# A two-layer backbone step: square sums between the spreads, late weights split in place, filler matmuls, and an earlier store

## The reference, cut to what matters

```python
for l in range(2):                                   # the same code for 128 context and 256 latent tokens
    h = rmsnorm(x) * (1 + scale1) + shift1
    q, k, v, xr, gr, ga, gb = split(h @ w_in)        # 5632 columns
    att = attention(q, k, v)                         # 8 heads of 128
    rnn = gelu(gr) * bidirectional_rg_lru(conv(xr))
    merged = sigmoid(ga) * (att @ w_attn_proj) + sigmoid(gb) * (rnn @ w_rnn_proj)
    x = x + gate1 * (merged @ w_out)
    h2 = rmsnorm(x) * (1 + scale2) + shift2
    x = x + gate2 * moe(h2)                          # 16 experts, top 2 in the best group of 4
y = rmsnorm(x) * final_norm_g
```

## Time and profile before

| what | value |
|---|---|
| median of 3 runs | 1584.49 us |
| the profiled execution | 1587.41 us, of it the span 1585.5 us |
| PE busy | 1485.0 us, 94% of the span |
| PEld, DVE, ACT, POOL busy | 75%, 70%, 58%, 10% |
| mean granted TensorE clock | 0.967 |
| chain that ended last | PE 79%, DVE 7%, ACT 4%, issue 4%, DMA 4%, POOL 1% |
| DMA, mean over the span | 235 GB/s |

### The profile page before, as it was taken

The page is one execution under the profiler, slowest core; times in us unless marked ns, Lnnn a source line. Parts: engine busy times, 40 slices in busy tenths (PEclk is TensorE's granted clock), DMA queues, the critical chain, the costliest instruction groups (busy, mean ns, idle before and its releaser), DMA issues.

```text
span 1585.5 us, 19352 instructions
## 1 busy us (share of the span) xinstructions
PE 1485.0 (94%) x7317; PEld 1195.4 (75%) x7317; DVE 1116.2 (70%) x1709; ACT 926.0 (58%) x1174; POOL 153.3 (10%) x209
## 2 busy tenths in 40 slices
PE   6999999989996999999979999999899599999996
PEld 3699866669875788888748998665898378888885
DVE  4447656765646999999852665776564689999996
ACT  1333579962224877778742245899321467787874
POOL 0100012200010000000230000221000200000002
PEclk8999999989997999999989999999899699999999
DMA  9455422124656999999744554112340789999993
GB/s 349 163 199 203 153 103 101 62 102 166 212 193 253 358 406 408 409 408 404 278 162 154 186 199 161 62 62 90 128 160 1 279 311 407 413 411 410 408 357 121
DMA packets 132708, 373.01 MB, mean 235 GB/s; under 512 B 9216, under 2 KB 12672, under 8 KB 132608
## 3 DMA queue, kind: packets, MB, share of 16 engines
q1 hardware_dynamic: 113728, 326.57, 54.9%
q0 software_dynamic: 10432, 25.18, 4.5%
q10 hardware_dynamic: 8448, 19.94, 3.2%
HBM read 351.71 MB, written 19.94 MB: 234 GB/s over the span
## 4 chain that ended last, share of the span: by engine, by line
PE 79%; DVE 7%; ACT 4%; issue 4%; DMA 4%; POOL 1%; SPq 0%; POOLq 0%; DVEq 0%; ACTq 0%
PE bank L522 24%; PE bank L820 19%; PE bank L511 10%; PE bank L826 10%; PE bank L532 2%; PE bank L712 2%; PE bank L792 2%; DMA ring<-in_w_ada 1%; PE bank L685 1%; PE bank L548 1%; DMA expert_rows<-gb 1%; PE bank L541 1%; PE bank L622 1%; PE bank L617 1%; DMA tmp<-expert_rows,posu 1%
## 5 line engine op out<-in xcount | busy, mean ns | idle before, releaser
L1838 DVE TENSOR_TENSOR spot_low<-spot,piece_high 128x2048 fp32r<-128x2048 f32 x192 | 434.1, 2287 | 32.8 <-ACT piece_high L1226 31.5
L1226 ACT ACTIVATE piece_high<-spot 128x2048 fp32r<-128x2048 f32 x192 | 366.9, 1917 | 46.6 <-PE bank L826 45.4
L820 PE MATMUL bank<-piece_high,ga_r 128*128 128x512 f32 x768 | 310.9, 405 | 4.7 <-ACT ga_r L1231 2.2
L820 PE MATMUL bank<-spot_low,ga_r 128*128 128x512 f32 x768 | 303.7, 395 | 0.0
L826 PE MATMUL bank<-piece_high,ga_r 128*128 128x512 f32 x768 | 211.6, 397 | 0.0
L511 PE MATMUL bank<-hT,ring 128*128 128x384 f32 x576 | 198.0, 499 | 9.6 <-ACT hT L1041 6.5
L522 PE MATMUL bank<-parts_r,ga_r 128*128 128x384 f32 x768 | 202.6, 345 | 0.0
L820 PEld LDWEIGHTS bank<-piece_high,ga_r 128*128 128x128 f32 x768 | 145.6, 190 | 39.0 <-ACT ga_r L1231 3.0
L511 PEld LDWEIGHTS bank<-hT,ring 128*128 128x128 f32 x576 | 109.2, 195 | 82.6 <-issue 11.3
L826 PEld LDWEIGHTS bank<-piece_high,ga_r 128*128 128x128 f32 x768 | 145.1, 189 | 34.8
L820 PEld LDWEIGHTS bank<-spot_low,ga_r 128*128 128x128 f32 x768 | 145.9, 190 | 31.0
(11 more groups left out here) (308 smaller groups left out, 2289.3 us busy)
## 6 DMA issues: line engine op xcount, KB each, us to landing
spot<-in_w_gate_up SPq DMA_DIRECT2D x128, 1024.0 KB, 8.0
spot<-in_w_down SPq DMA_DIRECT2D x64, 1024.0 KB, 8.3
ring<-in_w_ada SPq DMA_DIRECT2D x24, 2048.0 KB, 8.0
ring<-in_w_in SPq DMA_DIRECT2D x22, 2048.0 KB, 8.0
expert_rows<-gb ACTq DMA_DIRECT2D x28, 512.0 KB, 7.3
ring<-in_w_attn_proj SPq DMA_DIRECT2D x4, 2048.0 KB, 8.6
ring<-in_w_rnn_proj SPq DMA_DIRECT2D x4, 2048.0 KB, 8.3
ring<-in_w_out SPq DMA_DIRECT2D x4, 2048.0 KB, 8.0
```

The costliest lines, as they stand in the source:

```text
L820: pe.matmul(out[n], high[:, 2 * q + k, :], w[:, k, n * 512:(n + 1) * 512], start=(q == 0 and k == 0 and i == 0), stop=False)
L1226: ac.activation(highs[p % HIGHS], spots[u], ACT.Copy).then_inc(S("piece_high"), 1)
L1838: ve.tensor_tensor(spots_low[u], spots[u], highs[p % HIGHS].bitcast(F32), ALU.subtract)\
```

## The change

Six edits, five of them in both layers.

1. Late weights: the high part goes to one of four buffers (`spare` and three in `hT`), the low part is written over the chunk in its ring slot. `xc` is no longer used. A ring slot of a late chunk is released when the last product with it has ended, not when its low part is written.
2. End of attention: the first late high part moves into the loop, `lru_tables(15)` and `lru_root(15)` move behind `att_copy(23)` and the second high part; on DVE `one_minus_square(15)` moves behind the second low part.
3. `run_on`: ten float32 matmuls per layer into a bank that nobody reads: two of 384 columns before the ranks, four of 512 before `ids`, three before `xturn(0)`, one behind it.
4. Last expert: `copy_y(13)` and `store_y(13)` stand ahead of the high part of gate_up's last piece. `low_of(0)` stands between the combinations of rows, `low_of(1)` behind them.
5. Layer 0's tail: the squares and their sums stand ahead of the branch, the sum of group g - 3 behind the spread of group g. In the branch the squares are made again after each further block (a sixth PE step).
6. Layer 1's chunk "kv", and with it all loads behind it on SP, waits for the square sums (`ss_done`).

```diff
+LAG = 3
+LATE_HIGHS = 4
...
-                   [(part(hTf, 0), part(hTf, 1)), (part(hTf, 2), part(spare_r, 0)), (part(xcf, 0), part(xcf, 1))]]
+        late_high = [part(spare_r, 0)] + [part(hTf, i) for i in range(LATE_HIGHS - 1)]
+        ring_r = sb_r("ring")
...
-        def w_part(kind, n):
+        def w_high_part(kind, n):
 
             at = SPLIT_AT[kind, n]
-            return w_parts[at // EARLY][at % EARLY % PAIRS_OF_PARTS]
+            return w_parts[at % PAIRS_OF_PARTS][0] if at < EARLY else late_high[at % LATE_HIGHS]
+
+        def w_low_part(l, kind, n):
+
+            at = SPLIT_AT[kind, n]
+            if at < EARLY:
+                return w_parts[at % PAIRS_OF_PARTS][1]
+            s = CHUNK_SLOT[CHUNK_AT[(l, f"{kind}{n // 4}")]][0]
+            return ring_r[:, s, :].rearrange("p (k n) -> p k n", k=KT)[:, :, n % 4 * P:(n % 4 + 1) * P]
...
-                if g[1:] in SPLIT_AT:
+                if SPLIT_AT.get(g[1:], EARLY) < EARLY:
                     return S("w_low"), split_no(*g) + 1
             return S("gemm_done"), G_AT[g] + 1
...
+                if l and name == "kv":
+                    sy.wait_ge(S("ss_done"), 2 * l + 1)
...
+            def run_on(bank, times, width=512):
+
+                for _ in range(times):
+                    pe.matmul(bank[:, 0:width], ident, con[:, 256:256 + width], start=True, stop=True)
...
+                run_on(SB[1], 2, T)
                 bank = t_take((l, "rank", 0))
...
+                run_on(SB[1], 4)
                 bank = t_take((l, "ids", 0))
...
+                run_on(SB[1], 3)
                 xturn(0)
+                run_on(SB[1], 1)
...
                     mm.then_inc(S("group_done"), 1)
+                    if l + 1 < DEPTH and g >= LAG:
+                        square_sum(hT, g - LAG, slice(0, T), sq_base + KT + g - LAG + 1)
+                if l + 1 < DEPTH:
+                    for g in range(KT - LAG, KT):
+                        mm = square_sum(hT, g, slice(0, T), sq_base + KT + g + 1)
+                    mm.then_inc(S("ss_done"), 1)
...
                 one_more(0)
 
                 if l + 1 < DEPTH:
-                    for g in range(KT):
-                        mm = square_sum(hT, g, slice(0, T), sq_base + KT + g + 1)
-                    mm.then_inc(S("ss_done"), 1)
                     continue
...
+                    if i == 3 * KT - 1:
+                        high_part(EARLY)
...
-                    if i >= KT:
+                    if KT <= i < 3 * KT - 1:
                         lru_tables(i - KT)
                     if i >= 1:
                         att_copy(i - 1)
-                lru_root(15)
-                high_part(EARLY)
                 att_copy(23)
                 high_part(EARLY + 1)
+                lru_tables(15)
+                lru_root(15)
...
-                    piece_high(f"gu{e}", 3)
+                    if e < NE - 1:
+                        piece_high(f"gu{e}", 3)
                     if e >= 2:
                         copy_y(e - 2)
+                    if e == NE - 1:
+                        store_y(e - 2)
+                        piece_high(f"gu{e}", 3)
...
-                ac.activation(smx[:, 0, 7:8], ones[:, 0:1], ACT.Sqrt)
                 ac.wait_ge(S("blocks_known"), l + 1)
                 more = ac.value_load(nri[0:1, 0:1], min_val=0, max_val=MORE)
+                x_steps = 6 if l + 1 < DEPTH else 5
+                if l + 1 < DEPTH:
+                    for g in range(KT):
+                        ac.wait_ge(S("group_added"), l * KT + g + 1)
+                        ac.activation(hT[:, g, :], xT[:, g, :], ACT.Square).then_inc(S("sq_ready"), 1)
...
                 one_more(0)
+                ac.activation(smx[:, 0, 7:8], ones[:, 0:1], ACT.Sqrt)
...
-                one_minus_square(15)
                 low_part(EARLY)
                 att_split(HEADS - 1)
                 low_part(EARLY + 1)
+                one_minus_square(15)
                 scan(15)
...
-                for i in range(HELD):
-                    ve.wait_ge(S("y_copied"), l * NE + SENT + i + 1)
-                    low_of(i, (SB_pair, G_pair)[i], slot_gate[:, SENT + i:SENT + i + 1]).then_inc(S("held_low"), 1)
+                    if t:
+                        i = t - 1
+                        ve.wait_ge(S("y_copied"), l * NE + SENT + i + 1)
+                        low_of(i, (SB_pair, G_pair)[i], slot_gate[:, SENT + i:SENT + i + 1]).then_inc(S("held_low"), 1)
```

44 lines of the change are left out of this document (25 added, 19 removed).

## The result

The changed kernel takes 1569.68 us in the median of four runs (1568.08 to 1571.1). The kernel before took 1584.05 us in the same set (four runs, 1583.37 to 1587.31). The ratio is 0.9905, its 95% interval 0.9887 to 0.9923: 14.4 us are won where 24.5 were forecast, and the time lies 1.7 us outside the range of 1556.5 to 1568. The profiled execution took 1571.1 us, with a span of 1569.2 us against 1585.5 before. The 16.3 us between the two spans are what the traces can explain. The other 2 us are spread between executions: the profile of before lay 3.4 us over the median of this set, this one 1.4 us over its own.

The account below looks back on a forecast made before the run. PE is four fifths of the chain, so time is won only where it waits or runs at low clock. 10.4 + 7.65 + 1.75 + 4.7 = 24.5 us off 1587.41, less 2.9, gives 1560.0; eight in ten: 1556.5 to 1568.

Parts of the forecast that it names:

- End of attention: Late weights and reordered end of attention: first late product 4.4 us earlier, third 5.2 per layer, 10.4 us in all.
- the wait of 1.6 us: Ahead of the third late product, PE waits for its low part, delayed on DVE behind `scan(15)`: 1.6 us given back.
- Fillers: Routing and first expert: filler matmuls off the path keep PE's clock up, 4.3 + 3.35 = 7.65 us.
- lower bound of 2.7: Routing and first expert: if the fillers run cold and delay the first expert, 1.8 + 0.9 = 2.7 us remain.
- Edit 4: Layer tails: earlier store of expert 13 and moved `low_of` bring rows and spread sooner, 1.75 us per layer.
- Squares, sums and loads: Layer 0's tail: sums among the spreads, keys start at 813.9 when held weights land: 4.7 us, including 1.75 from the store.
- The sign that I had named: Ahead of layer 1's keys: PE waiting for a DMA would show the forecast right.
- (a): First expert: clock falls just as it starts, 4.55 us lost from the sum, 1564.6 us; chance 0.2.
- (b): End of attention gives little, half its gain lost: 5.2 us less, 1565.2 us; chance 0.12.
- (c): Late weight stream stalls PE 2.5 us per hand-over from landings of 16 us on; about 1611 us; chance 0.03.
- (d): Layer 0's tail gives nothing, its load landing in 13 us instead of 8: 1564.7 us; chance 0.05.
- The sign for "wrong" that I had named: Whole kernel: a total gain under 16 us would show the forecast wrong.

Follow-up runs that it names:

- run 5: Changed kernel without the ten filler matmuls per layer; 1569.9 us, ratio 0.9915 to the kernel before.
- run 6: Changed kernel with the old order at the end of attention, late weights still split in place with four high buffers; 1576.37 us, ratio 0.9959 to the kernel before.
- run 9: Changed kernel with DVE's low parts of expert 14's down and expert 15's pieces written in two half instructions; 1563.27 us, ratio 0.987 to the kernel before.
- run 10: Run 9 with expert 13's copy and store also put back where they stood before; 1561.69 us, ratio 0.9865 to the kernel before.
- run 11: Changed kernel with four filler matmuls between the last down product and the first transposes of both tails; 1565.46 us, ratio 0.9887 to the kernel before.
- run 12: Run 10 with five fillers instead of four ahead of `ids`; 1559.27 us, ratio 0.9852 to the kernel before.
- run 1: Changed kernel with expert 13's copy and store and both `low_of` put back where they stood; 1567.05 us, ratio 0.9903 to the kernel before.
- run 2: Changed kernel with only expert 13's copy and store put back where they stood; 1563.52 us, ratio 0.989 to the kernel before.
- run 3: Changed kernel with only both `low_of` put back behind the three combinations; 1567.41 us, ratio 0.9913 to the kernel before.
- run 4: Changed kernel with layer 1's loads no longer waiting for the square sums; 1568.31 us, ratio 0.9908 to the kernel before.
- run 7: Changed kernel with squares and sums behind the branch again, the loads' wait for the sums kept; 1571.86 us, ratio 0.9929 to the kernel before.
- run 8: Changed kernel with squares and sums behind the branch again and loads not waiting for the sums; 1574.39 us, ratio 0.9946 to the kernel before.

## Why the prediction was wrong

- **End of attention: right at its first step, a little high behind it.** The first late product came 4.3 us earlier (4.4 forecast). The 0.8 us more behind it aren't steady: +0.7 in layer 0, -0.4 in layer 1, where the clock fell behind a wait of 2.23 us that it had stood before. With 8.95 us for both layers it was within its bounds (8.8 to 11). The way there was partly another: the wait of 1.6 us that I forecast ahead of the third product never came, because the first product ran at half clock (granted 0.50 from 336 to 339, 5.6 us in place of 4.2) and the third low part was ready at 345.91, when PE came to it at 345.98.
- **Fillers: right in mechanism, in size partly by luck.** Layer 1 gave 3.3 us (3.35 forecast). Layer 0 gave 2.6 in the profile of the changed kernel, close to the lower bound of 2.7 that I had worked out for cold fillers, and 4.2 in the other traces (4.3 forecast). But 1.7 of those 4.2 run 5 has without any filler; against run 5 they bring 2.5 us in layer 0. I took it that none of them lies on the path, and in most traces the cold third group does, by about 0.9 us.
- **Edit 4: this step failed.** I wrote that with the store moved ahead "the six gathers behind it: the last rows land at 789.2 instead of 790.95", and so 1.75 us per layer. The rows came 1.9 us later against the experts instead, PE's wait grew from 1.97 to 3.83 us, and the transposes behind it ran cold: -2.7 and -2.0 us, and -0.7 in the spreads of layer 1. Of the 8.2 us between the two spans and my sum, this step is 8.9; the other steps make up for 0.7. I shifted the chain behind the store as a block, with each duration as it stood. Three of the six durations (those that start at 776.22, 782.68 and 784.96) were not the gathers' own but held waits for DVE, and in the page nothing said so: their release is given as "issue". Nor did I ask what the pushed-back high part does to DVE's list: it alone ends the first gather 0.7 us later. I also let the wait of PE grow or shrink without asking for the clock behind it, though I had done so everywhere else.
- **Squares, sums and loads: right in sign, sized by a wait that isn't there.** The weights were never held (I misread where the wait stands), so the keys were not bound by a load at 813.9; 5.3 us came behind the spread where 2.95 were forecast. The sign that I had named, PE waiting for a DMA ahead of the keys, didn't show; PE waited 5.65 us for ACT. The 5.5 us from the root to the keys were right (5.46).
- **Not priced: the square root's table in layer 1's tail.** With its preload behind the branch no other table is loaded in between, and the load of 1.28 us in the final norm is gone: 1.3 us won.
- **Rivals.** None of the four was it. (a) was wrong: the clock was up in the first expert, though it had fallen ahead of it. (b) was 12% and the end of attention gave 8.95 of 10.4. (c) didn't come: the weight stream never stalled PE. Its price didn't follow from its own slack either: with 5.5 us at a landing of 13.5, a stall needs more than 19.0 us, not 16, and the 18.6 us of the earlier trace rows would have cost nothing. (d)'s premise was the wait that I misread. The case that came, a moved store whose rows come no sooner, I had not priced; the durations of the six gathers in the trace of before would have raised the question. The sign for "wrong" that I had named, a total gain under 16 us, came true.

What stays open: why the first gather, which waits for the store, starts up to 7.4 us after the store's issue in the changed kernel and 3.7 to 5.0 with the late order; the trace shows single packets of it until 767.5, but not why they are last. What decides whether the clock falls behind a wait of about 2 us. And the 2 us by which the medians move less than the profiled spans.

## What to carry to other kernels

Before a chain is shifted, ask of each duration in it whether it is the instruction's own: a gather on GpSimd that takes 0.94 us alone and 1.9 to 2.5 beside a long two-input VectorE instruction is a wait, and its place against VectorE's list decides. An earlier store need not land earlier while the DMA engines are full: with it the first gather started 15.5 to 16.2 us behind `xturn(15)` in 13 of the 16 tails with whole low parts and at 14.0 to 14.2 in three, against 14.9 to 15.4 with the late one. And every wait of PE that a change lengthens must be priced twice: the wait, and the clock behind it.

## What the runs showed of the hardware

- A gather that starts inside a VectorE instruction with both inputs in SBUF ends 0.81 us behind it: so in the gathers with the 2.29 us instruction and with the 1.23 us one that are quoted here. None took less than 0.93 us.
- The row behind PE's branch cost 3.38 and 3.42 us with weight loads in flight, and 0.46 to 0.6 us without. ACT's cost nothing in either case.
- Layer 1's late products hold the same wait of 2.22 or 2.23 us for DVE in all fourteen traces. Behind it PE ran on at full clock in seven (before, runs 5, 6 and 9 to 12) and at half clock in seven (the changed kernel, runs 1 to 4, 7 and 8). From the first late product to the end of that layer's late products it took 114.4 us in runs 5, 9, 10 and 12 (115.5 in run 11) and 115.8 to 116.0 in the seven at half clock. Single profiles differ by 1.5 us for this alone.
